# Six gate steps move from the projections' block into the attention

## What is computed

```python
q, g = jnp.split(h @ w_in, 2, axis=-1)
q = rmsnorm(q.reshape(B, L, SB_HEADS, SB_DH), q_g)
o = stick_breaking(q, k_all, v_all, pos, k_pos, bias).reshape(B, L, SB_W)
return (jax.nn.silu(g) * o) @ w_out
```

## Time and profile before

| | us |
|---|---|
| median of 3 runs (1898.43 to 1899.19) | 1898.54 |
| the profiled execution: span from its first to its last instruction | 1896.1 |
| what lies around the span, against the median | 2.4 |
| PE busy | 1810.2 (95%) |
| PE weight loads busy | 1427.6 (75%) |
| DVE busy | 1054.8 (56%) |
| ACT busy | 810.6 (43%) |

### The profile page before, as it was taken

The page is one execution under the profiler, slowest core; times in us unless marked ns, Lnnn a source line. Parts: engine busy times, 40 slices in busy tenths (PEclk is TensorE's granted clock), DMA queues, the critical chain, the costliest instruction groups (busy, mean ns, idle before and its releaser), DMA issues. The chain is left out here.

```text
span 1896.1 us, 27878 instructions
## 1 busy us (share of the span) xinstructions
PE 1810.2 (95%) x10103; PEld 1427.6 (75%) x10103; DVE 1054.8 (56%) x1971; ACT 810.6 (43%) x1678; POOL 81.0 (4%) x140
## 2 busy tenths in 40 slices
PE   5999999999999999999999999999989988999998
PEld 2678787878787878677878767888777766676677
DVE  4663535353535353634446345755178788888852
ACT  3742323232333333313325223533367677878620
POOL 2000000000000000000000000011000000000000
PEclk8999999999999999999999999999999999999999
DMA  9221213130304040583424563223323253553252
GB/s 323 84 92 58 92 57 96 53 124 24 126 22 148 0 148 25 178 267 96 134 56 172 203 210 114 82 92 112 109 60 84 79 166 99 157 153 126 57 177 95
DMA packets 184939, 215.54 MB, mean 114 GB/s; under 512 B 45352, under 2 KB 142560, under 8 KB 183809
## 3 DMA queue, kind: packets, MB, share of 16 engines
q1 hardware_dynamic: 171146, 167.17, 28.6%
q0 software_dynamic: 13696, 47.08, 6.5%
HBM read 165.39 MB, written 48.83 MB: 113 GB/s over the span
## 5 line engine op out<-in xcount | busy, mean ns | idle before, releaser
L469 PE MATMUL rt_acc<-rt_w_hi,rt_h_hi 128*128 128x512 f32 x504 | 203.3, 403 | 1.0 <-DVE rt_h_lo L1008 1.0
L471 PE MATMUL rt_acc<-rt_w_hi,rt_h_lo 128*128 128x512 f32 x504 | 197.1, 391 | 0.0
L470 PE MATMUL rt_acc<-rt_w_lo,rt_h_hi 128*128 128x512 f32 x504 | 196.5, 390 | 0.0
L1051 DVE TENSOR_TENSOR rt_by_cos<-rt_raw,rt_cos 128x256 f32<-128x256 f32 (+1 forms) x72 | 30.5, 424 | 243.9 <-ACT rt_raw L881 243.9
L2895 PE MATMUL kq_acc<-kq_w_hi,kq_h 128*128 128x512 f32 x384 | 153.7, 400 | 4.7 <-DVE kq_w_lo L2695 4.7
L2896 PE MATMUL kq_acc<-kq_w_lo,kq_h 128*128 128x512 f32 x384 | 150.7, 392 | 0.0
L2898 PE MATMUL kq_acc<-kq_w_hi,kq_h 128*128 128x512 f32 x384 | 150.7, 392 | 0.0
L892 ACT COPY rt_qk_t<-rt_tr 128x256 f32<-128x256 f32 (+1 forms) x72 | 26.0, 361 | 278.4 <-PE rt_tr L700 278.4
L1931 ACT COPY pa_w_t<-pa_wt 128x512 f32<-128x512 f32 (+2 forms) x160 | 86.8, 543 | 72.4 <-PE pa_wt L1749 69.5
L2044 DVE TENSOR_TENSOR_SCAN pa_after_key<-pa_keep 128x128 f32<-128x128 f32 (+3 forms) x128 | 101.7, 815 | 19.9 <-ACT pa_take L1913 8.7
L471 PEld LDWEIGHTS rt_acc<-rt_w_hi,rt_h_lo 128*128 128x128 f32 x504 | 94.6, 188 | 20.6
(11 more groups left out here) (396 smaller groups left out, 4104.0 us busy)
## 6 DMA issues: line engine op xcount, KB each, us to landing
ro_a_raw<-retained SPq DMA_DIRECT2D x14, 1024.0 KB, 5.8
op_ada<-in_ada_w SPq DMA_DIRECT2D x8, 1024.0 KB, 12.8
rt_w_raw<-in_ret_w_in SPq DMA_DIRECT2D x16, 512.0 KB, 5.1
rt_w_raw<-in_ret_w_in SPq DMA_DIRECT2D x8, 1024.0 KB, 8.0
rt_old<-in_state_ret SPq DMA_DIRECT2D x8, 1024.0 KB, 6.2
rt_g_raw<-in_ret_w_in SPq DMA_DIRECT2D x8, 1024.0 KB, 5.3
out_st_sample<-rt_new POOLq DMA_DIRECT2D x8, 1024.0 KB, 8.3
kq_w_raw<-in_sb_w_in SPq DMA_DIRECT2D x4, 2048.0 KB, 8.9
```

Of the source, the lines that this page charges most:

```text
L469: nc.tensor.matmul(dst, h_hi[:, k, cols], w_hi[:, k, :], start=k == 0, stop=False)
L470: nc.tensor.matmul(dst, h_hi[:, k, cols], w_lo[:, k, :], start=False, stop=False)
L471: last = nc.tensor.matmul(dst, h_lo[:, k, cols], w_hi[:, k, :], start=False, stop=k == KD - 1)
```

## The change

Six prompt steps of the first half of the gates (chunk 6, tiles 2 to 7) are no longer made in the projections' block. They become the first six of now 15 steps in the attention; the block keeps the sample step and tiles 0 and 1 (`KQ_GATES = 2`). Chunk 6 must then be the chunk that stays in buffer 1, so the buffers change parity (`at(c)`). Chunk 7 is no longer loaded and split ahead: after the sixth step SP loads it into `w_raw[1]`, and ScalarE and VectorE split it in four parts in iterations 33 to 36, in which no slices run (`PAUSE`). A period is 16 places, filled over 13. The steps end at pieces 0, 7, 12, 17, 23, 28, then 40, 46, 51, 56, 62, 67, 72, 78, 83. The new sample rows are turned at 94 to 96, the pages at 98 to 157, and the sample pieces stand at 106, 117, 122, 139, 146, 151, 157 and 161.

```diff
+        S_AT = (106, 116, 122, 139, 145, 151, 156, 160)
         for b in range(DB):
-            at = S_FIRST + S_EVERY * b
+            at = S_AT[b]
...
-        SLICES = NT * KD
-        START, FIRST_SLOT, PERIOD, FILL = KD, 3, 24, 19
+        g_steps = [(0, t) for t in range(KQ_GATES, NPT)] + [(1, t) for t in range(NT)]
+        NG, SWITCH = len(g_steps), NPT - KQ_GATES
+        SLICES = NG * KD
+        START, FIRST_SLOT, PERIOD, FILL, PAUSE = KD, 3, 16, 13, 21
...
                 return START
+            turn = (SWITCH - 1) * PERIOD
+            if q > turn:
+                q = max(turn, q - PAUSE)
...
+        G_SWITCH = min(p for p in range(NPC) if steps_done_at(p) == [SWITCH - 1])
+        G_SPLIT, G_PARTS = G_SWITCH + 5, 4
+        GS = KD // G_PARTS
...
-        new_slots = {p: n for n, p in enumerate(free_slots(HALF - 9, 3))}
+        new_slots = {p: n for n, p in enumerate(free_slots(G_END + 5, 3))}
...
             def load_g(pair):
...
-                if pair == PAIRS // 2:
+                if pair:
                     for n in range(2):
-                        sp.wait_ge(g_stored[n], 16 * len(range(n, NT, 2)))
+                        sp.wait_ge(g_stored[n], 16 * pair)
...
+                if p == G_SWITCH + 1:
+                    sp.wait_ge(made, SWITCH)
+                    src = t_in["sb_w_in"][0].rearrange("(k p) n -> p k n", p=P)[:, :, 3 * NB:4 * NB]
+                    sp.dma_start(proj.w_raw[1][:], src).then_inc(g_w_loaded, 16)
...
-                if p == HALF + 10:
+                if p == G_END + 9:
...
+                    if i == SWITCH and k % GS == 0:
+                        pe.wait_ge(g_lo_s, k // GS + 1)
...
+            def split_g(q):
+                act.wait_ge(g_w_loaded, 16)
+                part = slice(GS * q, GS * (q + 1))
+                nc.scalar.copy(proj.w_hi[1][:, part, :], proj.w_raw[1][:, part, :]).then_inc(g_hi_s, 1)
...
-                for t in steps_done_at(p):
-                    open_gates(t)
+                for i in steps_done_at(p):
+                    open_gates(i)
+                if 0 <= p - G_SPLIT < G_PARTS:
+                    split_g(p - G_SPLIT)
...
+            def rest_g(q):
+                dve.wait_ge(g_hi_s, q + 1)
+                part = slice(GS * q, GS * (q + 1))
+                nc.vector.tensor_tensor(proj.w_lo[1][:, part, :], proj.w_raw[1][:, part, :], proj.w_hi[1][:, part, :].bitcast(F32),
+                                        ALU.subtract).then_inc(g_lo_s, 1)
...
-KQ_STEPS = 7 * NT
+KQ_GATES = 2
+KQ_STEPS = 6 * NT + 1 + KQ_GATES
...
-                  (w_qg, 2, None, ACT.Silu, None), (w_qg, 3, None, None, None)]
+                  (w_qg, 2, None, ACT.Silu, None)]
...
-        AHEAD_AT = 2
+        AHEAD_AT = 0
...
+        def at(c):
+
+            return (c + 1) % 2
```

More of the change, by code:

```diff
@@ L1629, in _, with store_gates @@
         def _(pool):
-            def store_gates(t):
-                pool.wait_ge(g_ready, t + 1)
-                half = ps.g_cols[NB:2 * NB, :]
+            def store_gates(i):
+                pool.wait_ge(g_ready, i + 1)
+                n, t = g_steps[i]
+                half = ps.g_cols[n * NB:(n + 1) * NB, :]
                 if t < NPT:
-                    dst, src = half[t // 2 * P:(t // 2 + 1) * P, t % 2 * NB:(t % 2 + 1) * NB], g_out[:, t % 2, :]
+                    dst, src = half[t // 2 * P:(t // 2 + 1) * P, t % 2 * NB:(t % 2 + 1) * NB], g_out[:, i % 2, :]
                 else:
@@ L1653, in _ @@
                 pool.wait_ge(stored[n], 16 * len(range(n, PAIRS - 1, 2)))
-                pool.wait_ge(g_stored[n], 16 * len(range(n, NT, 2)))
+                pool.wait_ge(g_stored[n], 16 * len(range(n, NG, 2)))
         @block.tensor
@@ L2004, in _ @@
             for n in range(2):
-                act.wait_ge(g_stored[n], 16 * len(range(n, NT, 2)))
+                act.wait_ge(g_stored[n], 16 * len(range(n, NG, 2)))
             for k in range(KD):
@@ L2064, in ready_samples @@
             def ready_samples():
-                dve.wait_ge(made, NT)
+                dve.wait_ge(made, NG)
                 nc.vector.memset(sa.after_key[:], 1.0).then_inc(cleared, 1)
@@ L2116, in gate_at, with finish_gates @@
                     gate(pieces[p].u)
[L2118 to L2122, removed]
+            def finish_gates(i):
+                if i == NG - 1:
+                    dve.wait_ge(made, NG)
+                    dve.wait_ge(g_stored[i % 2], 16 * (i // 2))
                     nc.vector.tensor_copy(y, acc[0:NS, 0, :]).then_inc(upper, 1)
@@ L2148, in _ @@
                     gate_at(p - 4)
-                for t in steps_done_at(p):
-                    finish_gates(t)
+                for i in steps_done_at(p):
+                    finish_gates(i)
+                if 0 <= p - G_SPLIT < G_PARTS:
+                    rest_g(p - G_SPLIT)
                 if p == G_END + 3:
@@ L2482, in shared_kv_and_queries @@
                   (w_qg, 0, ps.q_gain, None, q_out), (w_qg, 1, ps.q_gain, None, q_out),
-                  (w_qg, 2, None, ACT.Silu, None), (w_qg, 3, None, None, None)]
+                  (w_qg, 2, None, ACT.Silu, None)]
         SWITCH, GATES = 4, 6
-        steps = [(c, t) for c in range(len(chunks) - 1) for t in ([NPT, *range(NPT)] if c == GATES else range(NT))]
+        steps = [(c, t) for c in range(len(chunks)) for t in ([NPT, *range(KQ_GATES)] if c == GATES else range(NT))]
         assert len(steps) == KQ_STEPS
-        AHEAD_AT = 2
+        AHEAD_AT = 0
         SPLITS = 4
@@ L2640, in split @@
             def split(c, q):
-                raw = w_raw[c % 2] if c else proj.first_raw
+                raw = w_raw[at(c)] if c else proj.first_raw
                 if c:
-                    act.wait_ge(w_loaded[c % 2], 16 * (c // 2 + c % 2))
+                    act.wait_ge(w_loaded[at(c)], 16 * ((c + 1) // 2))
                 part = slice(KS * q, KS * (q + 1))
-                nc.scalar.copy(w_hi[c % 2][:, part, :], raw[:, part, :]).then_inc(hi_s, 1)
+                nc.scalar.copy(w_hi[at(c)][:, part, :], raw[:, part, :]).then_inc(hi_s, 1)
             for q in range(SPLITS):
@@ L2691, in split @@
             def split(c, q):
-                raw = w_raw[c % 2] if c else proj.first_raw
+                raw = w_raw[at(c)] if c else proj.first_raw
                 dve.wait_ge(hi_s, SPLITS * c + q + 1)
                 part = slice(KS * q, KS * (q + 1))
-                nc.vector.tensor_tensor(w_lo[c % 2][:, part, :], raw[:, part, :], w_hi[c % 2][:, part, :].bitcast(F32),
+                nc.vector.tensor_tensor(w_lo[at(c)][:, part, :], raw[:, part, :], w_hi[at(c)][:, part, :].bitcast(F32),
                                         ALU.subtract).then_inc(lo_s, 1)
```

58 lines of the change are left out of this document (30 added, 28 removed).

## The result

The change makes the kernel slower. The median after is 1910.91 us (1910.12 to 1911.35), that of before beside it 1898.87, ratio 1.0059 with a 95% interval of 1.0047 to 1.0071. I had forecast 1890.5 and a range up to 1903. The profiled execution's span is 1908.5 us for 1896.1, +12.4.

The account below looks back on a forecast made before the run. TensorE was taken to bound the projections' block, and VectorE's 2.12 us beat the attention's pieces without slices, TensorE those with them. -32.6 + 22 + 2 + 0.5 = -8.1 us from 1898.54 gave 1890.5, range 1880 to 1903.

Parts of the forecast that it names:

- The removed steps: Projections' block: six steps of 24 matmuls taken out, all on the only busy engine, TensorE: -32.6 us.
- The growth of the first half: Attention, pieces 0 to 83: the added slices, step ends and split lengthen it by 22 us, range 9 to 36.
- two accounts: Attention's first half: TensorE's added slices less its idle time, 17.0 us; VectorE's six new step ends plus split, 21.1.
- The third account: Attention's first half: TensorE sets the period, 2.88 us a piece; 76 pieces with slices grow by 22 us.
- The moved sample pieces: Attention: page turns moved later make ten pieces dearer, +3.3 us, and freed pieces give back 1.3: +2, range 0 to 5.
- The weights' load: Attention: the 2 MB load lands before the split at piece 33, with 1.7 us of margin: 0, or 3 to 5 us.
- the end of the stage: Attention's end: output weights and attended rows load later, with 1 to 2 us left: +0.5 us, range 0 to 4.
- TensorE has no room left: Attention: each moved slice shows its full 0.74 us; with each new end stopping TensorE, 1904 to 1910 us; chance 0.16.
- The waits overlap: Attention: VectorE's pauses coincide with its catching up, growth only 9 to 17 us: 1877.5 to 1885.5; chance 0.18.
- A transfer comes late: Attention: the 2 MB load, sample pages or final rows arrive late, 3 to 6 us on top: 1893.5 to 1897; chance 0.16.
- The sign that I named: Attention's first half: TensorE's idle time after would be near 5 us if it has no room, over 12 if not.

Follow-up runs that it names:

- e4: The changed kernel without sigmoid, product and TensorE's wait at the ends of the prompt gate steps, zeros stored as gates: 1885.40 us.
- e5: The kernel before without sigmoid, product and waits for the prompt gate steps in the attention: 1890.82 us.
- e10: The changed kernel with VectorE's product of a gate step one piece later, and without the load and split of chunk 7: 1886.32 us.
- e1: The kernel before with only the sample pieces and the turns of new rows and pages moved as in the change: ratio 1.0002.
- e11: The kernel before with its nine gate steps in periods of 16 places filled over 13, not 24 over 19; no step or split added: 1909.87 us.
- e12: e11 without sigmoid, product and the waits for them in the prompt steps, zeros stored as gates: 1897.58 us.
- e3: The changed kernel with six matmuls of no use in each of the four pieces where chunk 7's weights are split: 1913.16 us.

## Why the prediction was wrong

**The removed steps** (-32.6): right. The block is 32.5 us shorter, and no preparation of the attention showed behind it (the first slice starts 2.98 us behind the block's last matmul in both kernels, and piece 0 12.7 us behind that). It ends at 1331 and not at 1329, 1.7 of it for the block's later start.

**The growth of the first half** (+22): this step failed. It is 40.3, far over the 28 above which I had called the forecast wrong. I had two accounts, 17.0 and 21.1, and took them for two views of one cost, near the 22 of the third. They were two costs:

- TensorE's slices, 35.5 less the idle time there was: 17.0. Measured 23.2 - 4.1 = 19.1 (e4 against e5, less the split by e10), or 21.3 if the 2.2 us are added that the moved sample turns gave back in the same stretch (e1).
- VectorE's hand-overs 16.2 and split 4.9: 21.1. Measured 17.1 and 4.1: 21.2.

The sum of the two accounts, 38.1, is near the 40.3 (42.5 with those 2.2 us). That each comes so near is in part luck. From e5 to e4 TensorE's busy time grew by 28.5 us and not by 35.5, and its idle time fell by 5.2 (13.8 to 8.6) and not by 18.5. And the 16.2 were six new ends at 2.7 us each, VectorE's whole idle time. In before the ends cost far less than that: 5.0 in pieces 0 to 84 and 8.2 in all, for 20.8 us of idle time. After, the stretches with the six new ends are 9.5 us dearer, and 7.3 us came in the stretch of the one end behind the pause, which had no price of its own in my sum.

My reading of it: a pause of VectorE can be hidden as long as TensorE has idle time to catch up with, and slices put into that idle time leave the pauses to be paid. e11 and e12 bear this out in sum, at one spacing more (the same eight hand-overs 4.1 us dearer, no step added), but not piece by piece: in pieces 7 to 28 an end costs no more at the close spacing. The low end of my range for this term, 9, and its high end, 36, were both made of one account at a time.

The third account, by what a piece costs, came out right in the packed pieces: I had 2.88 us a piece at the close spacing, and pieces 7 to 28 take 61.1/21 = 2.91, a growth of 5.9 as that gives. It failed where I carried it over. I said that the split mostly fills TensorE's free pieces; pieces 28 to 40 grew by 8.9 us. And pieces 66 to 84, which had no slices before, went from 43.8 to 60.0, 3.3 a piece: there slices (8.7 of it by e4 and e5) and hand-overs (7.5) add up most plainly.

Not all ends are alike either. The first end behind the split waits 6.69 us: VectorE has finished a short piece (256 columns), and TensorE is still making the step's last slices. Of the hand-overs' 22.1 us, 6.2 lie in its stretch. How much of that the lower clock there adds stays open: in the first half the granted clock is 0.96 in after and 0.99 in e4, so hand-overs and time at 1.2 GHz come together, and e3, whose own matmuls cost time, doesn't part them.

**The moved sample pieces** (+2, range 0 to 5): right. +3.9 in pieces 84 to 167, less the 2.2 that pieces 66 to 84 gave back in e1, are 1.7; e1's stretches give 1.2, its median none.

**The weights' load and the end of the stage** (0 and +0.5): right. SP issues the load at 1425.55, and the first cast of it on ScalarE starts at 1437.89 without a wait:

```profile
1425.55 0.37 SPq L1613 DMA_DIRECT2D kq_w_raw<-in_sb_w_in  x1
```

```profile
1437.89 1.05 ACT L1988 CAST kq_w_hi<-kq_w_raw 128x1024 fp32r<-128x1024 f32 x1
```

The attended rows are issued at 1788.63, and their cast at 1799.54 lists no wait; what follows piece 167 is no longer than before:

```profile
1788.63 1.73 SPq L1638 DMA_DIRECT2D ao_a_raw<-attended  x3
```

```profile
1799.54 0.94 ACT L2022 CAST ao_a_hi<-ao_a_raw 128x896 fp32r<-128x896 f32 x1
```

**The rivals.** "TensorE has no room left", with each new end stopping it, gave up to 1910 and came nearest, at a chance of 0.16. It was right in that TensorE is full without the hand-overs (e4). It was wrong in what an end costs: it put 6 x 1.04 = 6.2 us on the six new ends, while all ends together became 17.1 dearer, 7.3 of it at the one end behind the pause, and it had no split. Its total was near by luck: it let all 35.5 us of the slices show, where 19.1 did. "The waits overlap" is the opposite of what happened: the waits grew from 20.8 to 51.1. "A transfer comes late" didn't occur.

**The sign that I named** for TensorE's room was ill chosen: idle time "near 5 us if it has no room, over 12 if not". It is idle 256.50 - 236.42 = 20.1 us in the first half, and that is not room: without hand-overs 8.6 are left (234.40 - 225.82). The idle time is part of the loss.

## What to carry to other kernels

When work is moved into the idle time of one engine, ask what that idle time was doing: if it lets the engine make up for pauses at hand-overs, the moved work and the pauses are both paid, and accounts made engine by engine may have to be added and not met in the middle. An instruction that waits for another engine's fresh result belongs one stage later in an in-order engine's program, behind the work that is ready: here that one move was worth 20 us in one kernel and 7 in the other, more than the change it was found by. And an experiment on the spacing alone, with the amount of work left as it is, is a cheap test of whether a stretch is overfilled.

## What the runs showed of the hardware

A stretch of matmuls can be full while its weight loads are busy 80% of it: 58.06 us of 58.20 for matmuls, 46.59 for weight loads (e4, pieces 7 to 28). And in after TensorE's granted clock was 0.86 over pieces 28 to 40, where it was busy 31.16 of 37.40 us and waited 1.17 and 1.05 us for VectorE's products. The missing slices alone don't do it: e10 has the same pause, is busy 26.08 of 27.50 us there, and has the full clock. 24 matmuls of no use brought it back to 1.00 in after (e3), without a gain in time.
